# A two-block transformer kernel on one core: experts' rows gathered as quarters of 256 features on 128 partitions and turned on VectorE

## What is computed

```python
N_EXPERTS, TOP_K, D_FF_EXPERT = 32, 4, 1024
logits = xt @ router_w + router_b
top_logit, top_idx = lax.top_k(logits, TOP_K)
top_gate = softmax(top_logit)
...
xb = xt[tok]                        # an expert's tokens, gathered
hid = xb @ w1[e] + b1[e]            # 1024 -> 2048
glu = minimum(hid[:, :D_FF_EXPERT], 7.0)
lin = clip(hid[:, D_FF_EXPERT:], -7.0, 7.0)
act = glu * sigmoid(1.702 * glu) * (lin + 1.0)
y = (act @ w2[e] + b2[e]) * gate    # 1024 -> 1024, then summed per token
```

## Time and profile before

| | us |
|---|---|
| median of 3 executions | 2682.08 (2679.12 to 2686.24) |
| profiled execution, its own time | 2676.38 |
| its span in the trace | 2674.7 |
| TensorE busy | 2543.1 (95%) |
| VectorE busy | 964.0 (36%) |
| ScalarE busy | 432.5 (16%) |
| POOL busy | 129.7 (5%) |

### The profile page before, as it was taken

One profiled execution on the slowest core, in us unless ns is written; L12 is line 12 of the kernel. 1 busy time (PEld: TensorE's weight loads), 2 busy tenths in 40 slices (PEclk: granted clock), 3 DMA queues, 4 the chain that ended last, 5 costly groups with the idle time before them and its releaser, 6 DMA issues.

```text
span 2674.7 us, 49323 instructions
## 1 busy us (share of the span) xinstructions
PE 2543.1 (95%) x20809; PEld 1426.8 (53%) x20809; DVE 964.0 (36%) x1840; ACT 432.5 (16%) x864; POOL 129.7 (5%) x188
## 2 busy tenths in 40 slices
PE   5999999797999999999999999799999998999999
PEld 2444787644344444444444444435556644888888
DVE  5563655413222222222222222424145322555451
ACT  2411143412001010000000000011124301111100
POOL 0000000000000000010000010300000000000000
PEclk8999999897999999999999999799999999999999
DMA  7432000106999999999999999661110101121221
GB/s 270 154 126 95 3 2 1 65 1 270 370 410 410 408 409 407 408 410 409 407 406 408 409 409 408 238 217 63 53 74 32 32 32 63 63 95 63 87 65 53
DMA packets 142654, 555.42 MB, mean 208 GB/s; under 512 B 14672, under 2 KB 50544, under 8 KB 93152
## 3 DMA queue, kind: packets, MB, share of 16 engines
q1 hardware_dynamic: 127088, 515.22, 49.3%
q0 software_dynamic: 12896, 36.48, 4.1%
q10 hardware_dynamic: 2576, 2.36, 0.3%
HBM read 537.25 MB, written 16.78 MB: 207 GB/s over the span
## 4 chain that ended last, share of the span: by engine, by line
PE 91%; DVE 4%; ACT 2%; DMA 1%; issue 1%; POOL 0%; SPq 0%; ACTq 0%; POOLq 0%; DVEq 0%
PE psum L2477 25%; PE psum L2061 20%; PE psum L2494 13%; PE psum L2767 10%; PE psum L2796 5%; PE psum L2219 2%; PE psum L2391 2%; PE psum L2686 2%; PE psum L2663 1%; PE psum L2464 1%; PE psum L2333 1%; PE psum L2359 1%; PE psum L2641 1%; PE psum L2651 1%; DVE arena L1304 1%
## 5 line engine op out<-in xcount | busy, mean ns | idle before, releaser
L2477 PE MATMUL psum<-ring,arena 128*32 128x512 f32 x6144 | 668.0, 594 | 3.6 <-ACT arena L1005 3.6
L2477 PEld LDWEIGHTS psum<-ring,arena 128*32 128x32 f32 x6144 | 196.7, 110 | 446.4 <-issue 446.0
L2494 PE MATMUL psum<-ring,arena 128*32 128x256 f32 x6144 | 339.8, 381 | 2.1 <-DVE arena L1696 2.1
L2061 PE MATMUL psum<-hT,ring 128*128 128x512 f32 x752 | 337.3, 605 | 3.3 <-ACT hT L821 3.3
L2494 PEld LDWEIGHTS psum<-ring,arena 128*32 128x32 f32 x6144 | 197.4, 110 | 132.8 <-issue 3.6
L2061 PEld LDWEIGHTS psum<-hT,ring 128*128 128x128 f32 x752 | 143.6, 194 | 179.9 <-issue 177.9
L1680 DVE TENSOR_TENSOR arena<-psum,hT 128x768 f32<-128x768 f32 x32 | 30.6, 957 | 536.1 <-PE psum L2477 536.1
L1011 ACT ACTIVATE arena<-arena 128x768 f32<-128x768 f32 x32 | 27.1, 846 | 844.3 <-DVE arena L1682 844.3
L2767 PE MATMUL psum<-ring 128*128 128x256 f32 x704 | 159.1, 379 | 0.5 <-ACT arena L807 0.5
L2767 PEld LDWEIGHTS psum<-ring 128*128 128x128 f32 x704 | 133.7, 190 | 19.1 <-ACT arena L807 0.9
L2767 PE MATMUL psum<-hT,ring 128*128 128x256 f32 x528 | 122.6, 383 | 7.9 <-DVE hT L1265 7.1
(11 more groups left out here) (390 smaller groups left out, 2592.9 us busy)
## 6 DMA issues: line engine op xcount, KB each, us to landing
ring<-in_exp_w SPq DMA_DIRECT2D x384, 1024.0 KB, 15.6
ring<-in_w_in SPq DMA_DIRECT2D x15, 2048.0 KB, 8.1
ring<-in_ada_w SPq DMA_DIRECT2D x12, 2048.0 KB, 8.1
ring<-in_w_ffn_in SPq DMA_DIRECT2D x22, 1024.0 KB, 7.7
expert_rows<-arena POOLq DMA_DIRECT2D x128, 96.0 KB, 6.0
ring<-in_w_ffn_out SPq DMA_DIRECT2D x8, 1408.0 KB, 6.8
ring<-in_w_out SPq DMA_DIRECT2D x2, 2048.0 KB, 7.9
ring<-in_w_o SPq DMA_DIRECT2D x2, 2048.0 KB, 8.0
```

The source lines that it names most:

```text
L2061: ins = mm(dst, l, r, start=(i == 0), stop=(i == len(parts) - 1))
L2477: ins = mm(bank[s][q * SG:(q + 1) * SG, :], XG[:, k, s * SG:(s + 1) * SG], w[:, q], start=(k == 0), stop=(k == KD - 1))
L2494: ins = mm(bank[3 + s // 2][q * SG:(q + 1) * SG, (s % 2) * 256:(s % 2 + 1) * 256], aT2k[:, s, k // 2, k % 2, :], w2_slot(k)[:, q * 256:(q ...
```

## The change

The rows are written to `h2_d` with their features in another order (quarter, then tile of 128, then 32 within it), and `h2_d` is read as 2048 rows of 256 features. A slot of group g, number s in it, and quarter q live on partition 32 q + s: three gathers, one for each group, fetch 128 rows of 1 KB each. The number of such a row is 4 times the token plus the quarter, so the token constants are multiplied by 4 and `look_up` adds the quarter. `mark_slots` writes a 0/1 matrix by the number in the group, four times beside each other for the quarters, and a right-hand side (`OH_ID`) that holds the token number in the column of the slot's group; `split_slots` works out group and number once before the loop. TensorE's `turn_rows` and ScalarE's `take_turned` are gone. VectorE's new `turn_rows` turns `XR` to `XG` in 32x32 blocks; it stands before `activations(e+1)` and waits for the gathers of e+2 and for the end of `hidden(e+1)`. `hidden` waits for it by `gx_sb`, and so does the next gather.

```diff
-    put("token", np.concatenate([np.concatenate([i[:, None], np.full((P, 1), t * P)], 1) for t in range(NT)], 1))
+    put("token", QT4 * np.concatenate([np.concatenate([i[:, None], np.full((P, 1), t * P)], 1) for t in range(NT)], 1))
+    put("quarter", row // SG)
...
-        XR = A(0, 2)[0:CAP, :]
+        XR = A(0, 2)[:, 0:GROUPS * 256].rearrange("p (g n) -> p g n", g=GROUPS)
+        h2_quarters = h2_d.rearrange("t (q n) -> (t q) n", q=QT4)
+        h2_split = h2_tok.rearrange("p t (q k r) -> p t k q r", q=QT4, k=KD)
...
-                pool.wait_ge(gx_mm, j * TURNS + (n + 1))
+                pool.wait_ge(gx_sb, j * TURNS + (n + 1))
                 pool.sem_inc(pool_turn, 1)
-                pool.indirect_dma_start(XR, None, h2_d, bass.IndirectOffsetOnAxis(ap=slot_token[0:CAP, 0:1], axis=0)).then_inc(rows_in, 16)
-                pool.wait_ge(rows_in, j * (16 * LOOKS) + n * 16 + 16)
+                for g in range(GROUPS):
+                    pool.indirect_dma_start(XR[:, g, :], None, h2_quarters, bass.IndirectOffsetOnAxis(ap=slot_token[:, g:g + 1], axis=0))\
+                        .then_inc(rows_in, 16)
+                pool.wait_ge(rows_in, (j * LOOKS + n) * (16 * GROUPS) + 16 * GROUPS)
...
-            def take_turned(j, n):
-                act.wait_ge(gx_mm, j * TURNS + (n + 2))
-                for i in range(2):
-                    ins = act.activation(XG[:, 4 * i:4 * i + 4, :].rearrange("p k s -> p (k s)"), bank[5 + i][:, 0:4 * CAP], ACT.Copy)
-                ins.then_inc(gx_sb, 1)
...
                 for t in range(NT):
-                    ins = dve.tensor_scalar(OH[:, t, :], const("iota", CAP), POS[:, t, bass.ds(n, 1)], None, ALU.is_equal)
+                    dve.tensor_scalar(OH[:, t, :].rearrange("p (q s) -> p q s", q=QT4), const("iota", SG)[:, None, :].to_broadcast([P, QT4, SG]), SLOT_IN[:, t, bass.ds(n, 1)], None, ALU.is_equal)
+                    ins = dve.scalar_tensor_tensor(out=OH_ID[:, t, :, :], in0=const("iota", GROUPS)[:, :, None].to_broadcast([P, GROUPS, 2]),
+                                                   scalar=SLOT_GROUP[:, t, bass.ds(n, 1)], op0=ALU.is_equal, op1=ALU.mult,
+                                                   in1=token[:, t, None, :].to_broadcast([P, GROUPS, 2]))
...
+            def turn_rows(j, n):
+                dve.wait_ge(rows_in, (j * LOOKS + n) * (16 * GROUPS) + 16 * GROUPS)
+                dve.wait_ge(w1_free, (j * EXPERTS + n) * (QT4 * KD) + QT4 * KD)
+                dve.transpose(XG.rearrange("p k (g s) -> p g k s", g=GROUPS), XR.rearrange("p g (k r) -> p g k r", k=KD)).then_inc(gx_sb, 1)
...
                     spread_bias()
+                    turn_rows(j, e + 2)
                     activations(j, e + 1)
...
-                    ins = mm(bank[7][0:CAP, 0:2], OH[:, t, :], token[:, t, :], start=(t == 0), stop=(t == NT - 1))
+                    ins = mm(bank[7][:, 0:2 * GROUPS], OH[:, t, :], OH_ID[:, t, :, :],
+                             start=(t == 0), stop=(t == NT - 1))
...
-            def turn_rows(j, n):
-
-                pe.wait_ge(rows_in, j * (16 * LOOKS) + n * 16 + 16)
-                for c in range(KD):
-                    ins = pe.transpose(bank[5 + c // 4][:, (c % 4) * CAP:(c % 4 + 1) * CAP], XR[:, c * P:(c + 1) * P], ident[0:CAP, 0:CAP])
-                ins.then_inc(gx_mm, 1)
```

More of the change, by code:

```diff
@@ L56 @@
                   level=6 * HD, eye=HD, hsel=P,
-                  iota=P, causal=P, cmp_bias=4 * 32, cmp_mask=4 * 32, inv_freq=32, expert=EXPERTS, token=2 * NT, eps=4)
+                  iota=P, causal=P, cmp_bias=4 * 32, cmp_mask=4 * 32, inv_freq=32, expert=EXPERTS, token=2 * NT, quarter=1, eps=4)
 HEAD_TILES = 8
@@ L328, in program @@
         b1_in, w1_free, w2_free = (sem(n) for n in ("b1_in", "w1_free", "w2_free"))
-        oh_ready, idx_mm, idx_f, idx_sb, gx_mm, gx_sb, glu_ready, lin_ready, sig_ready, act_ready = (sem(n) for n in (
-            "oh_ready", "idx_mm", "idx_f", "idx_sb", "gx_mm", "gx_sb", "glu_ready", "lin_ready", "sig_ready", "act_ready"))
+        oh_ready, idx_mm, idx_f, idx_sb, gx_sb, glu_ready, lin_ready, sig_ready, act_ready = (sem(n) for n in (
+            "oh_ready", "idx_mm", "idx_f", "idx_sb", "gx_sb", "glu_ready", "lin_ready", "sig_ready", "act_ready"))
         aT_sb, ye_sb = (sem(n) for n in ("aT_sb", "ye_sb"))
@@ L420, in program @@
         Y = wide(12)
-        OH = A(22).bitcast(BF16)[:, 0:NT * CAP].rearrange("p (t s) -> p t s", t=NT)
+        OH = A(22)[:, 0:256].bitcast(BF16)[:, 0:NT * P].rearrange("p (t s) -> p t s", t=NT)
+        OH_ID = A(22)[:, 256:320].bitcast(BF16)[:, 0:NT * 2 * GROUPS].rearrange("p (t g i) -> p t g i", t=NT, g=GROUPS)
+        SLOT_GROUP = A(23)[:, 0:136].rearrange("p (t e) -> p t e", t=NT)
+        SLOT_IN = A(23)[:, 136:272].rearrange("p (t e) -> p t e", t=NT)
         hid_psum = psum[:, 0:GROUPS * T].rearrange("p (s i n) -> p s i n", s=GROUPS, i=2)
@@ L448, in program @@
         n_pass = sb("n_pass", [P, 2], I32)
-        slot_token = small[:, 2:3].bitcast(U32)
-        slot_f = small[:, 0:1]
+        slot_token = small[:, 8:8 + GROUPS].bitcast(U32)
+        slot_f = small[:, 0:GROUPS]
         choice_at = small[:, 48:64]
@@ L983, in _ @@
                 for i in range(2):
-                    take(("ht", t, i), h2_tok[:, t, i * T:(i + 1) * T], ACT.Copy)
+                    take(("ht", t, i), h2_split[:, t, 4 * i:4 * i + 4], ACT.Copy,
+                         bank[plan.bank(("ht", t, i))][:, :].rearrange("p (k q r) -> p k q r", k=4, q=QT4))
             for t in range(NT):
@@ L1644, in _ @@
             dve.sem_inc(aT_sb, 1)
+            dve.sem_inc(gx_sb, 1)
             dve.wait_ge(npass_ready, 1)
@@ L1648, in _ @@
             LINKS = 4
-            CHOICE_LINKS = 5 + NT * (TOP_K - 1)
+            CHOICE_LINKS = 8 + NT * (TOP_K - 1)
             def bias_arrived(j, e):
@@ L1704, in _ @@
             with dve.Fori(0, passes) as j:
+                split_slots(j)
                 for n in range(2):
@@ L1707, in _ @@
                     look_up(j, n)
+                turn_rows(j, 0)
                 bias_arrived(j, 0)
@@ L1711, in _ @@
                 spread_bias()
+                turn_rows(j, 1)
                 activations(j, 0)
@@ L1719, in _ @@
                 ins.then_inc(choice_chain, 1)
-                dve.wait_ge(choice_chain, j * CHOICE_LINKS + 1)
+                dve.wait_ge(choice_chain, j * CHOICE_LINKS + 4)
                 dve.tensor_reduce(choice_at, picks, AX.X, ALU.add).then_inc(choice_chain, 1)
-                dve.wait_ge(choice_chain, j * CHOICE_LINKS + 2)
+                dve.wait_ge(choice_chain, j * CHOICE_LINKS + 5)
                 dve.tensor_scalar(choice_in, choice_at, 0.0, float(CAP - 1), ALU.max, ALU.min).then_inc(choice_chain, 1)
-                dve.wait_ge(choice_chain, j * CHOICE_LINKS + 3)
+                dve.wait_ge(choice_chain, j * CHOICE_LINKS + 6)
                 dve.scalar_tensor_tensor(out=by_tile(GTMP[:, 0:NT * TOP_K]), in0=TOPF[:, :, 0:TOP_K], scalar=float(CAP),
@@ L2504, in _ @@
                 hidden(j, 0)
-                turn_rows(j, 1)
                 number_slots(j, 2)
```

25 lines of the change are left out of this document (13 added, 12 removed).

## The result

| | before | after |
|---|---|---|
| median, us | 2681.93 (2679.12 to 2686.24, 4 runs) | **2651.99** (2646.73 to 2653.22, 4 runs) |
| after / before | | **0.9885** [0.9873, 0.9897] |
| the profiled execution's own time | 2676.38 | 2653.22 |
| TensorE busy | 2543.1 | 2513.9 |

The change makes the kernel 30 us faster.

A forecast was written before the change was run, and what follows sets the result against it. TensorE sets the loop's pace at 32.31 us a turn, with the DMA engines close behind at 32.83. Head +2.7, transposes -25.1 and late weights +8.4 sum to -14 us: 2668 us from 2682, range 2655 to 2711.

The forecast's parts named there:

- W: How late the expert loop's weight loads run once their reserve is used up: 8.4 us added to the time.
- the head: The part ahead of the loop, where nothing covers: splitting, marking and two more gather issues against cheaper turning, net +2.7 us.
- G: The gather's price on the DMA engines in each turn of the loop: 2.02 us before, forecast 1.7 us after.
- TensorE sets the pace: TensorE bounds the expert loop at 32.31 us a turn; removing its transposes saves 0.81 us in each of 31 turns, 25.1 us.
- The reserve of weights: In the loop, weights land 29.2 us at most before lateness; about 5 us of TensorE's gain fits before DMA decides.
- The formula: Lateness of the loop's loads: W = 27 x (30.81 + G - 31.50) - (28.4 - 9.5), if positive.
- The rows of full speed: Expert-row gathers on 128 partitions, evidence for the free-gather rival: G at most 1.39 us, -22 us, 2660; chance 0.16.
- 27 packets an engine: The new gather's packet count on each DMA engine; data alone, 24 an engine at 0.049 us, cost 1.18 us.
- packet price: Rival: each gather packet costs its turn between two reads, up to G 5.4 us, +86 us; chance 0.14, partly slower 0.12.
- The port estimate: Unequal partition halves in the 96-partition gather cause 0.31 of the 1.09 us lost, which would go; sum then -17 us.
- POOL's schedule: Three gathers leave POOL 2.5 us later, rows land about 1023, store done near 1032; fits with 3 and 5 us spare.
- ScalarE and VectorE: In the loop, two ScalarE copies fewer and a VectorE block transpose of 0.97 us more, all hidden: no effect on time.

The follow-up runs named there:

- e2: The changed kernel with eight transposes of constants put back on TensorE between the two layers, results unused: 2683.18 us, ratio 1.0004.
- e1: The kernel before without TensorE's eight transposes and ScalarE's two copies a turn, the gather as it was: 2675.01 us, ratio 0.9982.
- e3: The changed kernel with its 1 KB rows fetched by four gathers on 96 partitions instead of three on 128: 2679.98 us, ratio 1.0001.
- e5: The kernel before with its gather of 4 KB rows on 112 partitions instead of 96: 2682.59 us, beside 2682.21 of the kernel before.
- e10: The changed kernel with every gather issued twice, the second three only after the first three have landed: 2687.92 us (one run).
- e4: The kernel before with its gather of 4 KB rows on 128 partitions instead of 96: 2686.49 us (one run).
- e6: The changed kernel with six gathers of 128 rows of 512 B instead of three of 1 KB, the same bytes: 2710.81 us (one run).
- e7: The changed kernel with every gather of 1 KB rows issued twice, the second time to an unread region: 2707.12 us, ratio 1.0090.
- e8: The changed kernel with three gathers of 128 rows of 512 B, half of each row left out: 2650.91 us (one run).

## Why the prediction was wrong

The forecast was -14 us, measured are -30. Of the 16 us between them 8.4 are W, the waits for late weights that never came; 6.8 are TensorE's turn, which got 1.03 us shorter and not 0.81; 1.3 are the head; and the last store took 0.8 back. With G right and the rest as forecast the time would have been 2660, inside the range. It is the undersized saving on TensorE that put it below 2655.

- **"TensorE sets the pace", and the transposes are on its path: right. Their size, 0.81 us, was a term that failed.** I took 1027.31 - 1026.50 = 0.81 us, from the start of the transposes to the start of the second layer. But the transposes' own row starts late. A first layer takes 20.62 us until the second can start, so without them the second layer would have started at 1026.38, 0.12 us before their row begins; from layer to layer they cost 0.93 us (0.95 in e2). The numbering, which I left at 0.34, got shorter by 0.1. In all 1.03 us instead of 0.81, 32 us instead of 25.1. The right reading was from the start of one layer to the start of the next, less the layer's own 10.6 and 20.6 us.
- **The reserve of weights, about 29 us, and what it hides: right in mechanism.** It explains e1, e3, e5 and e10, each with a landing that stands still at 28 to 29 us. As for size: of the 0.95 x 31 = 29.5 us of its transposes e1 kept 5 and lost 25. The formula gives 17.0 with its 31.50 and 32.83, and 22.7 with the 31.36 and 32.9 measured: 27 x 1.54 - 18.9.
- **G = 1.7 us: the step that failed most, with 8.4 of the 16 us.** "I take half of the loss as gone." It was 1.00 us. I had named both suspects, the 96 partitions and two reads at once, and split the loss between them (half of 1.09 is 0.55, not 0.52, so even that sum should read 1.73), because no row had a gather on 128 partitions beside weights. e3, e4, e5 settle it: all of the loss goes with the 96 partitions. The rows of full speed, to which I gave 0.16 as a rival, were the better guide.
- **"27 packets an engine": wrong.** The 144 packets of the gather's window are 48 of under 512 B and 96 of 2 to 8 KB, which carry the 0.39 MB: 4 KB each, four rows in a packet, 6 an engine for the data. e6's window shows the same with 512 B rows: 192 packets, of which 96 lie between 2 and 8 KB. The "packet price" rival, which had 0.26 with its milder half, had no base. The Trainium skill, "DMA: Bandwidth & Descriptors", SWDGE vs HWDGE vs iDMA, which has descriptors put together to about 4096 B, agrees with both windows; I should have given it more than a sentence at the end of a rival.
- **W = 8.4 us: 0.** By the formula with G = 1.00 and the turn 31.28: 27 x 0.53 - 18.9 is negative. The DMA engines are still slower than TensorE by 0.53 us a turn, but the loop ends with about 6 us of reserve left (28.4 - 22.6).
- **The port estimate.** By the Trainium skill, "SBUF — State Buffer", DMA port swizzle, I estimated that 0.31 of the 1.09 us lost came from the unequal halves. All of the 1.09 went. With 112 partitions the halves are 64 and 48, a smaller imbalance, and the loss was at least as large (e5). Bytes per half don't explain it. What a gather on fewer partitions does in the engines stays open.
- **The head: +2.7, measured +1.4.** The splitting took 1.0 us (0.8 forecast). The marking up to the first gather's issue took 3.19 us against 3.13, where I had put 0.8 more. From the first gather to the rows' landing it is 5.85 us against 4.29, +1.6 instead of +2.5; the look-up and block transpose up to the first layer take 1.44 us where the turning took 2.68. **POOL's schedule: it fits, with more room.** The store, which waits for the rows to land, leaves 12.6 us after the start of the first layer (1013.28 - 1000.68). The forecast had the landing 17 us after it (1023 on the clock of a layer that starts at 1005.76); before, the store left 12.8 us after it. **ScalarE and VectorE: hidden,** as said; the block transpose takes 0.98 us. I said that the wait before the last second layer stays, and it does (2.13 us); that the last copy of sums would wait for the last store, 0.8 us more than before, I had missed.

## What to carry to other kernels

Measure a removed stage from the start of the work before it to the start of the work after it, not from its own row. Where a DMA stream runs beside a busy engine, work out both turns and the reserve between them: here neither the shorter TensorE turn (5 us) nor the cheaper gather (nothing) was worth much without the other, and together they gave 30 us. Where such a gather stands beside a saturated stream of weights, shape it to all 128 partitions even if that means fetching rows that nobody reads: it spares the DMA engines, which is worth time only where they set the pace (in e4 they did not). Keep few gathers under way at once.

## What the hardware showed that I had not expected

- A gather to 96 or 112 partitions beside a saturated stream of weights cost about 0.9 to 1.2 us of all 16 DMA engines beyond its bytes, with rows of 1 KB or 4 KB (370 and 373 GB/s in e3 and e5, against 419 to 422 with 128 partitions). It is not a price of the gather alone: ahead of the loop, with next to nothing else in the queues, the first gather of 96 partitions (649.09 us, before) and that of 128 (655.14 us, e4) both landed 4.2 us after their issue, and their packets took 1.34 us of all engines for 0.39 MB and 1.64 for 0.52 MB, 3.4 and 3.1 us a MB.
- Six gathers issued one behind the other stopped TensorE for about 1.5 to 1.7 us a turn of the loop, though it waited for no semaphore and kept its clock; four at once did not, nor three and then three. The cause isn't shown. It isn't late weights, whose landing stayed at 8 to 11 us, nor the bytes, which are twice as many in e7 as in e6 for about the same stop. Nor is it the number of gathers alone: in the last turn, with the weights already in, three gathers of 512 B rows (e8, 0.9 us) and four of 96 partitions (e3, gaps of up to 1.24 us) held TensorE up too, and three and four of 128 rows of 1 KB did not. Five at once weren't tried.
